# Attention scores from two 128-row products instead of three 64-row products

## The reference

```python
s = jnp.einsum('bqhd,bkhd->bhqk', qb, kb).astype(jnp.float32) * scale + bias[None]
s = jnp.where(valid[None, None, None, :], s, -jnp.inf)
p = jax.nn.softmax(s, axis=-1)
return jnp.einsum('bhqk,bkhd->bqhd', p, vb)
```

## Time and profile before

| | us |
|---|---|
| median of three runs | 1987.84 |
| the profiled execution, its own time | 1988.6 |
| its span | 1986.3 |
| TensorE busy | 1932.7 (97%) |
| VectorE busy | 1061.3 (53%) |
| GpSimd busy | 789.9 (40%) |
| ScalarE busy | 661.9 (33%) |

### The profile page before, as it was taken

One profiled execution on the slowest core, in us unless ns is written; L12 is line 12 of the kernel. 1 busy time (PEld: TensorE's weight loads), 2 busy tenths in 40 slices (PEclk: granted clock), 3 DMA queues, 4 the chain that ended last, 5 costly groups with the idle time before them and its releaser, 6 DMA issues.

```text
span 1986.3 us, 23385 instructions
## 1 busy us (share of the span) xinstructions
PE 1932.7 (97%) x9228; PEld 1610.6 (81%) x9228; DVE 1061.3 (53%) x1455; ACT 661.9 (33%) x960; POOL 789.9 (40%) x325
## 2 busy tenths in 40 slices
PE   7998999999999999999999999999999999999997
PEld 5776888888879798989888888888888878888886
DVE  5887862753785543434672534554555465335263
ACT  4224432222364232333432222233444433222232
POOL 4432444444453433333244444443122234444441
PEclk9999999999999999999999999999999999999998
DMA  5212332442231222222242323232222222323231
GB/s 170 91 64 64 118 105 96 138 147 86 85 106 64 85 85 85 85 85 72 76 126 85 106 85 106 92 98 95 63 70 67 65 78 92 102 90 106 85 106 42
DMA packets 165032, 182.15 MB, mean 92 GB/s; under 512 B 3504, under 2 KB 151232, under 8 KB 164816
## 3 DMA queue, kind: packets, MB, share of 16 engines
q1 hardware_dynamic: 158608, 169.36, 26.6%
q10 hardware_dynamic: 6336, 11.55, 1.9%
HBM read 178.76 MB, written 6.33 MB: 93 GB/s over the span
## 4 chain that ended last, share of the span: by engine, by line
PE 81%; DVE 7%; issue 6%; ACT 3%; POOL 2%; DMA 0%; ACTq 0%; DVEq 0%; POOLq 0%; SPq 0%
PE ps L380 27%; PE ps L382 26%; PE ps L381 26%; POOL w_lo L369 2%; DVE sum_of_squares L1099 1%; DVE xl L1083 1%; ACT w_hi L735 1%; ACT work L981 1%; PE ps L644 1%; DVE hid_lo L1157 1%; DVE x L1137 1%; DVE probs_t_lo L1544 0%; DMA x<-in_x_dram 0%; PE ps L458 0%; DVE cols L1529 0%
## 5 line engine op out<-in xcount | busy, mean ns | idle before, releaser
L369 POOL TENSOR_TENSOR w_lo<-raw,w_hi 128x1024 fp32r<-128x1024 f32 x320 | 789.5, 2471 | 1163.3 <-ACT w_hi L735 1163.3
L735 ACT ACTIVATE w_hi<-raw 128x1024 fp32r<-128x1024 f32 x320 | 336.2, 1057 | 736.9 <-PE ps L382 735.9
L380 PE MATMUL ps<-xh,w_hi 128*128 128x512 f32 x1408 | 556.8, 395 | 16.6 <-DVE xl L1083 15.6
L381 PE MATMUL ps<-xl,w_hi 128*128 128x512 f32 x1408 | 549.6, 390 | 0.0
L382 PE MATMUL ps<-xh,w_lo 128*128 128x512 f32 x1408 | 549.5, 390 | 0.0
L380 PE MATMUL ps<-hid_hi,w_hi 128*128 128x512 f32 x944 | 370.5, 392 | 14.9 <-issue 7.3
L382 PE MATMUL ps<-hid_hi,w_lo 128*128 128x512 f32 x944 | 368.1, 390 | 0.0
L381 PE MATMUL ps<-hid_lo,w_hi 128*128 128x512 f32 x944 | 368.1, 390 | 0.0
L380 PEld LDWEIGHTS ps<-xh,w_hi 128*128 128x128 f32 x1408 | 265.2, 188 | 75.7 <-issue 14.5
L381 PEld LDWEIGHTS ps<-xl,w_hi 128*128 128x128 f32 x1408 | 265.3, 188 | 56.0 <-issue 2.4
L382 PEld LDWEIGHTS ps<-xh,w_lo 128*128 128x128 f32 x1408 | 265.2, 188 | 55.7
(11 more groups left out here) (173 smaller groups left out, 1667.2 us busy)
## 6 DMA issues: line engine op xcount, KB each, us to landing
raw<-in_mlp_w_dram SPq DMA_DIRECT2D x64, 1024.0 KB, 5.4
raw<-in_ret_w_in_dram SPq DMA_DIRECT2D x24, 1024.0 KB, 5.1
raw<-in_att_w_in_dram SPq DMA_DIRECT2D x12, 1024.0 KB, 5.1
raw<-in_w_gate_dram SPq DMA_DIRECT2D x11, 1024.0 KB, 5.4
raw<-in_w_up_dram SPq DMA_DIRECT2D x11, 1024.0 KB, 5.4
raw<-in_w_in_dram SPq DMA_DIRECT2D x10, 1024.0 KB, 5.2
raw<-in_w_down_dram SPq DMA_DIRECT2D x8, 1024.0 KB, 5.0
raw<-in_ret_w_out_dram SPq DMA_DIRECT2D x8, 1024.0 KB, 5.0
```

Source lines behind the costliest of these rows:

```text
L369: nc.gpsimd.tensor_tensor(view[0], view[1], view[2].bitcast(F32), ALU.subtract).then_inc(w_lo, c.made(w_lo))
L380: nc.tensor.matmul(o, a[0], b[0], start=first, stop=False, skip_group_check=True)
L381: nc.tensor.matmul(o, a[0], b[1], start=False, stop=False, skip_group_check=True)
L735: nc.scalar.activation(view[0], view[1], ACT.Copy).then_inc(w_hi, c.made(w_hi))
```

## The change

The high part of a unit is made in two instructions of 64 partitions, and so is the low part. For queries, `q_hi` now holds the even head (high part in partitions 0 to 63, low part in 64 to 127) and `q_lo` the odd head (low part in 0 to 63, high part in 64 to 127). For keys the even head's parts stand in `k_hi` and `k_lo` in partitions 0 to 63, the odd head's in a new tile `k_odd` in partitions 64 to 127. Four DMAs per tile (`copy_k`, issued by ScalarE) then copy each part to the other 64 partitions, so that each key part stands twice. A product with `k_hi` over 128 rows gives high x high plus low x high; one with `k_lo` gives high x low plus low x low.

TensorE waits for the copies of a tile at the first even head that uses it. `copy_k(t)` waits on ScalarE for the low parts of the keys. It stands, for tile 1, behind the high part of the mixed head in head 0 of a group, for tile 0 behind the same in head 2, ahead of the exponentials, and twice in the opening. The tiles `work` and `tap_w` are given up in part so that `k_odd` fits; no view of `work` used in attention moves.

```diff
+        with ExitStack() as early:
+            work = early.enter_context(nc.sbuf_tensor("work", [P, 8448], F32))
+            tap_w = early.enter_context(nc.sbuf_tensor("tap_w", [P, 4, 2, P], F32))
+        sb("work_in_attention", [P, 7176])
+        ko = sb("k_odd", [P, 4, SEQ], F32R)
...
                         if h % 2 == 0 and 0 in tiles:
                             pe.wait_ge(qk_ready, c.next(qk_ready, 2))
-                        t, rows = h % 4 // 2, slice(64 * (h % 2), 64 * (h % 2) + 64)
+                            pe.wait_ge(k_copied[h % 4 // 2], 64 * (h // 4 + 1))
+                        t = h % 4 // 2
+                        q = (qh, ql)[h % 2][:, t, :]
+                        k_hi, k_lo = (ko[:, t, :], ko[:, 2 + t, :]) if h % 2 else (kh[:, t, :], kl[:, t, :])
...
-                            mm = product(ps[:, bank, at:at + n], [v[rows, t, P * i:P * (i + 1)] for v in (qh, ql)],
-                                         [v[rows, t, 0:n] for v in (kh, kl)], True, True)
+                            nc.tensor.matmul(ps[:, bank, at:at + n], q[:, P * i:P * (i + 1)], k_hi[:, 0:n],
+                                             start=True, stop=False, skip_group_check=True)
+                            mm = nc.tensor.matmul(ps[:, bank, at:at + n], q[:, P * i:P * (i + 1)], k_lo[:, 0:n],
+                                                  start=False, stop=True, skip_group_check=True)
...
                     def qk_hi(n, later=0):
                         act.wait_ge(unit_taken, c.unit.value(-later))
-                        dst = (qh, kh)[n % 2]
-                        nc.scalar.activation(dst[:, n // 2, :], hval[:, n % 2, :], ACT.Copy).then_inc(hi_made, c.made(hi_made))
+                        even, odd = ((qh, ql), (kh, ko))[n % 2]
+                        nc.scalar.activation(even[0:64, n // 2, :], hval[0:64, n % 2, :], ACT.Copy)
+                        nc.scalar.activation(odd[64:P, n // 2, :], hval[64:P, n % 2, :], ACT.Copy).then_inc(hi_made, c.made(hi_made))
+
+                    def copy_k(t):
+                        act.wait_ge(qk_ready, c.next(qk_ready, 2))
+                        for a, b in ((kh[0:64, t, :], kh[64:P, t, :]), (kl[0:64, t, :], kl[64:P, t, :]),
+                                     (ko[64:P, t, :], ko[0:64, t, :]), (ko[64:P, 2 + t, :], ko[0:64, 2 + t, :])):
+                            act.dma_start(b.bitcast(F32), a.bitcast(F32)).then_inc(k_copied[t], 16)
...
                     for n in (2, 3):
                         qk_done(n)
                         qk_hi(n)
+                        if n == 2:
+                            copy_k(0)
                     v_unit(0)
+                    copy_k(1)
                     exps(0)
...
                         if s == 0:
                             qk_unit(3)
                             mixed_hi(h - 1)
+                            copy_k(1)
                             v_unit(0)
...
                         mixed_hi(h - 1)
+                        if s == 2 and not last_group:
+                            copy_k(0)
                         if h + 1 < ATT_HEADS:
                             exps(h + 1)
...
                     def qk_unit(n):
-                        hi, lo = ((qh, ql), (kh, kl))[n % 2]
                         scaled(hval[:, n % 2, :], scale=0.125 if n % 2 == 0 else 1.0)
                         dve.wait_ge(hi_made, c.next(hi_made))
                         dve.wait_ge(*c.own())
-                        V.tensor_tensor(lo[:, n // 2, :], hval[:, n % 2, :], hi[:, n // 2, :].bitcast(F32), ALU.subtract).then_inc(qk_ready, c.made(qk_ready))
+                        t, low, high = n // 2, slice(0, 64), slice(64, P)
+                        if n % 2 == 0:
+                            pairs = ((low, qh[high, t, :], qh[low, t, :]), (high, ql[low, t, :], ql[high, t, :]))
+                        else:
+                            pairs = ((low, kl[low, t, :], kh[low, t, :]), (high, ko[high, 2 + t, :], ko[high, t, :]))
+                        for rows, lo, hi in pairs:
+                            signal = qk_ready if rows is high else dve_step
+                            V.tensor_tensor(lo, hval[rows, n % 2, :], hi.bitcast(F32), ALU.subtract).then_inc(signal, c.made(signal))
```

More of the change, by code:

```diff
@@ L169, in build @@
         ptl = sb("probs_t_lo", [P, PACKED], F32R)
-        work = sb("work", [P, 8448])
         r_bc = sb("r_bc", [P, SEQ])
@@ L177, in build @@
         cols = sb("cols", [P, 64])
-        tap_w = sb("tap_w", [P, 4, 2, P])
+        with ExitStack() as early:
[3 more added lines that the diff above has]
+        ko = sb("k_odd", [P, 4, SEQ], F32R)
         ps = ctx.enter_context(nc.psum_tensor("ps", [P, 8, SEQ], F32))
@@ L264, in build @@
         act_step = sem("act_step")
+        k_copied = [sem(f"k_copied{t}") for t in range(2)]
         turned_before_att = 4 * RET_HEADS if "ret" in phases else 0
+        qk_before_att = 2 * RET_HEADS if "ret" in phases else 0
         block = ctx.enter_context(nc.Block())
@@ L1000, in _ @@
                     qk_hi(1)
+                    c.of[qk_ready].n = qk_before_att
                     for n in (2, 3):
```

## The result

The changed kernel takes 1993.07 us, median of 9 runs (1991.95 to 1993.84), beside 1988.71 us (1983.19 to 1989.43) for 9 runs of the kernel before on the same chip: ratio 1.0034, 95% interval 1.0025 to 1.0043, so slower by 5 to 8.5 us. (The two medians lie only 4.4 us apart; the runs of the kernel before spread over 6 us.) The forecast was 1989.5, no change that can be told. The measured time is 0.6 us above the forecast's own range of 1986.5 to 1992.5 and inside the wide one of 1981 to 1999, and the case "slower by over 0.2%", to which the prediction gave 30%, is the one that came.

A forecast was written before the change was run, and what follows sets the result against it. TensorE was taken to bound heads 0 and the last group, the ScalarE-VectorE-GpSimd chain the first three groups' ends. +1.4 + 4.95 - 1.4 - 3.4 = +1.55 us gave 1989.5 us, range 1986.5 to 1992.5, wide 1981 to 1999.

The forecast's parts named there:

- slower by over 0.2%: Outcome for the whole kernel: a time above 1991.8 us; chance 30%.
- TensorE's saving, 1.36 us a head: Attention heads: fewer score products and a shorter mix save TensorE some 1.36 us each, 22 us over 16 heads.
- Delay per unit, 1.37 us: Query and key units: split high part adds 0.54 us, split low part 0.83, delaying VectorE 1.37 us; bounds 1.14 to 1.6.
- The saved time turns into waits for the maxima in heads 1 to 3: Each of the first three groups: TensorE waits ahead of tile 1's scores, nine heads in all, 0.5 to 2.3 us each.
- The opening, +1.4: Start of attention: first value unit starts 1.5 to 1.9 us later, some is won back, +1.4 us taken.
- Line 1529 misses its gap: Ends of the first three groups: VectorE's tiny negation again sits through GpSimd's second instruction; chain 1.43 to 1.85 us later.
- rival (a): Group ends: the negation slips in between GpSimd's two instructions and TensorE becomes the bound; 1984.3 us, chance 18%.
- A group end +1.65, less 0.7 for head 0, so +0.95 from one group end to the next: Chain ends 1.65 us later in three groups, +4.95; head 0 wins 0.7 in two groups, -1.4.
- The last group, -3.4: No query or key units there: two heads win 1.36 us each and the head before 0.7, -3.4 us.
- The transfers, 0, upper bound 2: The 32 key copies of 128 KB land before the scores need them: 0 us, at most 2 us in all.
- rival (d): Key copies come late, in the opening or by their issue ahead of the exponentials: +3 to +5 us, 1993.5, chance 8%.
- rival (c): TensorE's clock falls in nine new waits of 1 to 2 us: 13.5 us on top, 2003 us, chance 12%.

The follow-up runs named there:

- the maxima-first runs: Changed kernel with maxima of tiles 0, 2, 3 taken before VectorE's low halves: 1987.62 us with transfers behind the exponentials, 1986.31 us with transfers left in place.
- The split alone: Kernel before with only the high and low parts made in two 64-row instructions each, three products, no copies: 1994.51 us, ratio 1.0047.
- the filler run: Changed kernel with 11, 14 and 17 unused products ahead of tile 1's scores in heads 1 to 3 of the first three groups: 1991.41 us, ratio 1.0020.
- no transfers: Changed kernel without the copies of the keys and TensorE's wait for them: 1989.71 us, ratio 1.0018.
- negation on ScalarE: Changed kernel with the negation of the maxima moved from VectorE to ScalarE, ahead of the exponentials: 1988.99 us, ratio 1.0017.
- the sum of its two halves: Attention times of two edits of the kernel before, added: only split high and low parts (+7.89 us), only two 128-row products per tile (-8.52 us).

## Why the prediction was right in its mechanism and 4.5 us short

By its own steps:

- **TensorE's saving, 1.36 us a head**: right. Scores 1.04 instead of 1.76, mix 1.87 instead of 2.07. TensorE's busy time fell by 11.0 us only and not by the 15 or more that were to show it; matmuls at the lower clock count longer, and after has four falls more.
- **Delay per unit, 1.37 us**: 1.46 measured. VectorE's part is as forecast (0.82 against 0.83); ScalarE's is 0.64 against 0.54, as the two halves do not overlap. The two low halves follow each other in 0.72 us each, so the rule of the Trainium skill that the prediction weighed (VectorE: DVE Perf Modes) holds here too, at 0.11 us over the 0.61 of one instruction.
- **The saved time turns into waits for the maxima in heads 1 to 3**: right, nine waits of 1.43 to 2.19 us, and the maxima-first runs, in which they are gone or at most 0.5 us, show that they hang on the low halves ahead of the maxima.
- **The opening, +1.4**: +1.36, though by other parts. The value unit starts 1.99 us late; with the wait for the transfers head 0's scores are 3.33 us late, and the saved products of heads 0 and 1 take 1.96 back. The clock falls there in both traces, so it plays no part in the difference.
- **Line 1529 misses its gap**: right in every group (L1561 ends 0.03 us behind GpSimd's second product), so rival (a) did not come. The prediction had the two within 0.1 us and was right by a hair; the maxima-first runs show the other side. What it costs is shown by moving it: 1.6 us per group end in the kernel before.
- **A group end +1.65, less 0.7 for head 0, so +0.95 from one group end to the next**: this step failed. Measured: +2.24 to the first, then +2.11 and +1.86. Two things were wrong in it. The split alone costs 1.93 per group, just above the upper bound of 1.85 and not in the middle. And the 0.7 us won in head 0 do not survive: after goes from +3.60 to +2.79 by head 6's scores and is back on the same track at the next group end, +5.71 beside the +5.93 of the kernel that saves no product at all. A group whose end is set by the chain takes most of the chain's lateness, wherever TensorE stood in between. In the filler run, without clock falls in the groups, 1.33 and 1.69 came, so some 0.4 us per group of the saving do arrive there; in after the falls take them.
- **The last group, -3.4**: -1.56. In two traces of the changed kernel without a fall there it is -3.0 (no transfers) and -3.2 (negation on ScalarE). After's clock falls behind the 2.00 us wait ahead of the first output unit, and there nothing hides it: +1.49 us within that one unit (+6.87 to +8.36).
- **The transfers, 0, upper bound 2**: 0.5, in the opening, as far as the traces tell (rival (d) in small); the slowest took 6.7 us to land there. In the groups nothing waits for them, as forecast.
- **Clock falls, 0 in the sum (rival (c))**: this term should not have been nothing. After's falls behind the opening cost some 2.6 us, over half of the miss.

So 0.6 at the first group end, 1.16 and 0.91 at the next two, 1.84 in the last group: 4.5 us over the sum of 1.55 in attention. The miss of the median is 3.6 us (1993.07 against 1989.5); in the traces after was 1.97 us ahead when it came to attention, for which the forecast has no term. Rival (c) had the right cause and the wrong count and price: four falls came, behind waits of 2.19, 1.81, 2.17 and 2.00 us, but three of them cost 1.1 us together and only the one in TensorE's own stretch 1.5. The prediction argued against it that waits of 1.41 and one of 2.00 us had left the clock alone. One trace could not settle it. In the thirteen of this study 40 waits of 1.8 to 2.2 us stand between 1390 and 1600 us, and 26 had a fall behind them; the 2.00 us wait of the last group is in all thirteen, and had one in nine. The trace of before was one of the other four. No wait of 1.4 to 1.5 us in that stretch had one. The length of the wait is not all, though: in the opening one of 0.86 us, ahead of tile 1's scores of head 0, had a fall behind it in four of five traces.

Left open: why a wait is followed by a fall in one execution and not in the next, and how the 6.6 us between after and the sum of its two halves divide between the falls and the missing credit for TensorE's early arrival.

## What to carry to other kernels

Where two engines hand work to each other and are nearly equally long, as here, most of the time saved on one is spent waiting for the other, and the instructions that the saving adds to the other are paid at each handover. Price a group by its slowest chain from one handover to the next, and give little credit for what another engine wins in between. When a reordering helps, look whether it also moved an instruction into or out of a collision, as the maxima-first order did with the negation. Before comparing two traces count their clock falls. Before removing work from the busiest engine look for the instruction that its partner sits in (here a 4-column negation of 2.3 us, worth 4.4 us by moving it to an idle engine).

## What the runs showed of the hardware

- An instruction of 4 columns on VectorE from on-chip memory to on-chip memory stands until a GpSimd instruction with two operands from there is over: 2.18 us instead of 0.17, or 0.18 where it meets the end of the first of two. The maxima and the low part of the mixed head, with one operand in PSUM, run beside the same GpSimd product at their usual 0.28 to 0.69 us (1415.30 to 1417.55 in after). In the opening a low half with both operands in on-chip memory took 2.78 us instead of 0.69 (at 1363.13), also beside GpSimd. The Trainium skill, SBUF — State Buffer, section on the two separate sides, says that VectorE in a two-port mode or with two such operands and GpSimd lock each other out for a whole instruction; the traces agree, and the negation as one of the first kind fits it.
- Adding work to TensorE in its waits made the kernel faster (filler, 1.4 us by the trace, 2.8 by the ratio), and the mean clock of its runs went from 0.991 to 0.994.
- A fall of the clock costs 1.5 to 1.6 us where TensorE sets the pace, and some 0.2 to 0.5 us on average in the groups, where the chain does.
- 128 KB from one half of the partitions to the other land 2.2 to 2.7 us after issue in the groups, the same size from device memory 2.8; in the opening some took 4.8 to 6.7 us.
